# Casting a decoder's weights for scratch on GpSimd ahead of the first block

## The reference

```
xn   = rmsnorm(x) ; proj = xn @ w_in                 # 1024 -> 2048: B | C | xc | u
conv = B * causal_conv3(C * xc)                      # 512 channels
ssm  = GLU(Re(C_ssm h_t) + D u_t), h_t = Lbar h_{t-1} + Bbar u_t   # 32 groups, 64 states
x    = x + concat(conv, ssm) @ w_out                 # 1024 x 1024
hn   = rmsnorm(x)
x    = x + (silu(hn @ w_gate) * (hn @ w_up)) @ w_down   # 1024 x 2816, twice, and 2816 x 1024
y    = rmsnorm(x)
```

## Time and profile before

| | |
|---|---|
| time, median of 2 runs | 1637.3 us (1628.8 to 1645.8) |
| profiled execution | 1652.2 us |
| its span, slowest core (4) | 1650.3 us |
| spans of the 8 cores | 1614.6 to 1650.3 us |
| PE / DVE / ACT / Pool busy | 65% / 31% / 24% / 6% |
| mean rate of DMA | 114 GB/s |

### The profile page before, as it was taken

One profiled execution on the slowest core, in us unless ns is written; L12 is line 12 of the kernel. 1 busy time (PEld: TensorE's weight loads), 2 busy tenths in 40 slices (PEclk: granted clock), 3 DMA queues, 4 the chain that ended last, 5 costly groups with the idle time before them and its releaser, 6 DMA issues.

```text
span 1650.3 us, 23077 instructions; the slowest of 8 cores (1614.6 to 1650.3 us)
## 1 busy us (share of the span) xinstructions
PE 1066.9 (65%) x7740; PEld 560.6 (34%) x7740; DVE 511.4 (31%) x1071; ACT 391.5 (24%) x851; POOL 104.3 (6%) x187
## 2 busy tenths in 40 slices
PE   0343534345533357669897939898948899778992
PEld 0323324122210135343333624333724333453341
DVE  0117446235211154214515122532321551411111
ACT  0041433254421301331102151101132110132101
POOL 6010020200023000000000000000000000000000
PEclk9998656555555578869999959999977999998996
DMA  9450420678887321313344213345132334322442
GB/s 45 24 138 0 115 81 2 179 205 259 249 250 235 116 57 33 103 46 128 115 138 150 56 60 121 116 131 153 43 102 74 125 122 128 128 66 89 139 132 86
DMA packets 144387, 187.31 MB, mean 114 GB/s; under 512 B 13518, under 2 KB 106222, under 8 KB 144208
## 3 DMA queue, kind: packets, MB, share of 16 engines
q1 hardware_dynamic: 132800, 152.35, 32.3%
q0 software_dynamic: 11472, 33.49, 7.7%
HBM read 152.94 MB, written 32.85 MB: 113 GB/s over the span
## 4 chain that ended last, share of the span: by engine, by line
PE 40%; DMA 24%; DVE 16%; ACT 9%; issue 7%; POOL 2%; DVEq 1%; ACTq 0%; SPq 0%; POOLq 0%
PE bank L1011 13%; PE bank L1033 8%; DMA RGU<-wgu_s 4%; PE bank L749 3%; PE bank L914 3%; DMA STG<-wd 3%; ACT XN L672 3%; PE bank L925 3%; DMA STG<-wg 3%; DVE L2T L790 3%; DVE SETUPT L416 3%; DMA SETUPT<-ci 2%; PE bank L976 2%; DMA STG<-wu 2%; PE bank L771 2%
## 5 line engine op out<-in xcount | busy, mean ns | idle before, releaser
L1011 PE MATMUL bank<-SETUPT,RGU 128*128 128x512 bf16 (+1 forms) x1760 | 396.6, 370 | 103.1 <-ACT RGU L320 32.4
L1011 PEld LDWEIGHTS bank<-SETUPT,RGU 128*128 128x128 bf16 x1760 | 172.1, 104 | 326.4 <-issue 185.3
L749 PE MATMUL bank<-XTO,RWIN 128*128 128x512 bf16 (+1 forms) x640 | 166.4, 390 | 83.3 <-DMA RWIN<-win_s 24.8
L1033 PE MATMUL bank<-RW,ARENA 128*128 128x512 bf16 x748 | 183.0, 391 | 55.3 <-ACT RW L314 29.4
L1017 DVE TENSOR_TENSOR ARENA<-bank,SETUPT 128x512 bf16<-128x512 f32 (+1 forms) x110 | 66.3, 610 | 258.6 <-PE bank L1011 167.3
L749 PEld LDWEIGHTS bank<-XTO,RWIN 128*128 128x128 bf16 x640 | 64.1, 106 | 183.9 <-issue 144.1
L1033 PEld LDWEIGHTS bank<-RW,ARENA 128*128 128x128 bf16 x748 | 68.7, 98 | 168.5 <-issue 108.2
L691 PE MATMUL bank<-identb,XN 128*128 128x128 bf16 x272 | 34.4, 306 | 116.7 <-DVE XN L684 103.8
L1015 ACT ACTIVATE SETUPT<-bank 128x512 f32<-128x512 f32 (+1 forms) x110 | 57.0, 528 | 150.1 <-PE bank L1011 145.5
L976 PE MATMUL bank<-RW,ARENA 128*128 128x512 bf16 x272 | 67.0, 391 | 31.7 <-DVE RW L316 14.0
L1055 POOL DMA_DIRECT2D yp<-SETUPT x16 | 9.2, 578 | 1041.3 <-DVE SETUPT L1048 1039.8
(11 more groups left out here) (220 smaller groups left out, 1059.6 us busy)
## 6 DMA issues: line engine op xcount, KB each, us to landing
RGU<-wgu_s SPq DMA_DIRECT2D x88, 512.0 KB, 3.5
RW<-wd_s SPq DMA_DIRECT2D x176, 128.0 KB, 2.2
RWIN<-win_s SPq DMA_DIRECT2D x64, 256.0 KB, 2.7
STG<-wg SPq DMA_DIRECT2D x22, 512.0 KB, 7.4
STG<-wu SPq DMA_DIRECT2D x22, 512.0 KB, 6.0
wgu_s<-RGU POOLq DMA_DIRECT2D x22, 512.0 KB, 7.0
STG<-wd SPq DMA_DIRECT2D x44, 256.0 KB, 4.2
STG<-w_in SPq DMA_DIRECT2D x16, 512.0 KB, 5.0
```

What stands on the lines that cost most here:

```text
L749: E("pe", lambda e, bk=bk, wt=wt, k=k: e.matmul(bk[:, 0:NT], lhsT=wt[:, k, :], rhs=XTv[:, k, 0:NT], start=(k == 0), stop=(k == 7)), reads= ...
L1011: E("pe", lambda e, bk=bk, wt=wt, gi=gi, k=k: e.matmul(bk[:, 0:NT], lhsT=wt[:, gi, k, :], rhs=HT[:, k, 0:NT], start=(k == 0), stop=(k == 7 ...
L1033: E("pe", lambda e, bk=bk, wt=wt, f=f, t=t: e.matmul(bk[:, :], lhsT=ACT_[:, f * 512 + t * 128:f * 512 + (t + 1) * 128], rhs=wt[:, :], star ...
```

## The change

A section is added on Pool's queue, after the streams are set up and before any block is run. It loads in f32, casts on Pool and stores to scratch all of w_out (16 parts) and w_down (44 parts), and 15 of the 22 gate/up tiles (two parts each). Two staging buffers and one bf16 buffer for gate/up lie in the part of the arena that the decode block doesn't use; w_out and w_down parts are cast into RW's slots. The decode block then reads these weights from scratch, as the prompt blocks do, and casts only the first 7 gate/up tiles itself. The norm gain of the second norm is no longer multiplied into gate/up weights, but into HT at the transposes' eviction, in all blocks: eight `mul` instead of two `copy` on ACT per 128 tokens. The memsets of `prep_part1` and `prep_part3` go from Pool to DVE. Cut to its core:

```diff
-            Vx(lambda e: e.memset(BDR, 0.0), [], [b_bd], "pool")
+            Vx(lambda e: e.memset(BDR, 0.0), [], [b_bd])
...                                                 (11 memsets more, alike)
         def lookahead(stream, first, reqs, depth):
-            q = [stream.get(first, *reqs[i]) for i in range(min(depth, len(reqs)))]
+            fl = first if isinstance(first, list) else [first] * len(reqs)
+            q = [stream.get(fl[i], *reqs[i]) for i in range(min(depth, len(reqs)))]
...
+        GU_BG = 7
+        AR3 = ARENA[:, 0:4096].rearrange("p (r c) -> p r c", c=256)
+        bgst = [AR3[:, 0:8, 64:192], AR3[:, 8:16, 64:192]]
+        bggu = AR3[:, 0:16, 192:256].bitcast(BF16).rearrange("p (g k) c -> p g k c", g=2)
...
+        for key, pf, sap in wo_reqs():
+            bg_parts.append(("w", key, sap, pf(r_w.t[0])[0][1], 0, 1))
+        for key, pf, sap in wd_reqs():
+            bg_parts.append(("w", key, sap, pf(r_w.t[0])[0][1], 0, 1))
+        for key, pf, sap in gu_reqs()[GU_BG:]:
+            prt = pf(r_gu.t[0])
+            bg_parts.append(("g", key, sap, prt[0][1], 0, 2))
+            bg_parts.append(("g", key, sap, prt[1][1], 1, 2))
+
+        def bg_load(q):
+            kind_, key, sap, src_ap, pi, npart = bg_parts[q]
+            i = q % 2
+            if len(src_ap.shape) == 3:
+                view = bgst[i]
+            else:
+                view = bgst[i][:, 0:src_ap.shape[1] // 128, :]
+                src_ap = src_ap.rearrange("p (a c) -> p a c", c=128)
+            E("pool", lambda e: e.dma_start(out=view, in_=src_ap), writes=[b_bgst[i]], chan=bgst_ch[i])
+            return view
+
+        bg_views = {0: bg_load(0)}
+        for q in range(len(bg_parts)):
+            if q + 1 < len(bg_parts):
+                bg_views[q + 1] = bg_load(q + 1)
...
+            if kind_ == "w":
...
+                E("pool", lambda e, dst_ap=dst_ap, view=view: e.tensor_copy(out=dst_ap, in_=view),
+                  reads=[b_bgst[q % 2]], writes=r_w.b[si])
...
+                E("pool", lambda e, sap=sap, t=t: e.dma_start(out=sap, in_=t[:]), reads=r_w.b[si], writes=[sbuf],
+                  chan=r_w.sch[si])
+            else:
+                E("pool", lambda e, pi=pi, view=view: e.tensor_copy(out=bggu[:, pi, :, :], in_=view),
+                  reads=[b_bgst[q % 2]], writes=[b_bggu])
+                if pi == npart - 1:
...
+                    E("pool", lambda e, sap=sap: e.dma_start(out=sap, in_=bggu), reads=[b_bggu], writes=[sbuf],
+                      chan=bggu_ch)
...
+                        for kk in range(4):
+                            k = hh * 4 + kk
+                            E("act", lambda e, bk=bk, kk=kk, k=k, t=t: e.mul(
+                                out=DST[:, k, t * 128:(t + 1) * 128], in_=bk[:, kk * 128:(kk + 1) * 128],
+                                mul=gain[:, k:k + 1]), reads=[bb, b_G], writes=[b_dst])
...
             if kind == "p" and bi == 0:
+                handover(b_bgst + [b_bggu], mixer_bufs + b_actf)
...
-            norm_transpose(nt, HT, b_ht, 4, xt, bx)
+            norm_transpose(nt, HT, b_ht, 4, xt, bx, gain=G2C)
...
+            wo_it = lookahead(r_w, False, wo_reqs(), 3)
...
+            gu_it = lookahead(r_gu, [first and f < GU_BG for f in range(NF)], gu_reqs(), 1)
...
+            wd_it = lookahead(r_w, False, wd_reqs(), 3)
```

More of the change, by code:

```diff
@@ L453, in prep_part1 @@
             (r0, i0) = CHN[0]
-            Vx(lambda e: e.memset(BDR, 0.0), [], [b_bd], "pool")
-            Vx(lambda e: e.memset(NBDI, 0.0), [], [b_bd], "pool")
-            Vx(lambda e: e.memset(r0, 0.0), [], [b_bl[0]], "pool")
-            Vx(lambda e: e.memset(i0, 0.0), [], [b_bl[0]], "pool")
+            Vx(lambda e: e.memset(BDR, 0.0), [], [b_bd])
+            Vx(lambda e: e.memset(NBDI, 0.0), [], [b_bd])
+            Vx(lambda e: e.memset(r0, 0.0), [], [b_bl[0]])
+            Vx(lambda e: e.memset(i0, 0.0), [], [b_bl[0]])
             for ci_ in range(2):
-                Vx(lambda e, ci_=ci_: e.memset(CHN[1][ci_], 0.0), [], [b_bl[1]], "pool")
+                Vx(lambda e, ci_=ci_: e.memset(CHN[1][ci_], 0.0), [], [b_bl[1]])
             for ee in range(2):
@@ L528, in prep_part3 @@
         def prep_part3():
-            E("pool", lambda e: e.memset(KT[:], 0.0), writes=[b_kt])
-            V(lambda e: e.memset(K0F, 0.0), "pool")
+            E("dve", lambda e: e.memset(KT[:], 0.0), writes=[b_kt])
+            V(lambda e: e.memset(K0F, 0.0))
             for ci_ in range(2):
                 for cj_ in range(2):
-                    Vx(lambda e, ci_=ci_, cj_=cj_: e.memset(CHN[ci_][cj_], 0.0), [], [b_bl[ci_]], "pool")
+                    Vx(lambda e, ci_=ci_, cj_=cj_: e.memset(CHN[ci_][cj_], 0.0), [], [b_bl[ci_]])
             (r0, i0) = CHN[0]
@@ L660, in build_nc, with wo_reqs, gu_reqs @@
         mixer_bufs = [b_xt] + b_mix + b_zg
+        def wo_reqs():
+            return [(("wo", k, half), (lambda t, k=k, half=half: [(
+                t[:, :], wout_d[k * 128:(k + 1) * 128, half * 512:(half + 1) * 512], None)]),
+                wout_s[k, :, half * 512:(half + 1) * 512]) for half in range(2) for k in range(8)]
+        def gu_reqs():
+            return [(f, (lambda t, f=f: [
+                (t[:, 0, :, :], wg_d[:, f * 128:(f + 1) * 128].rearrange("(k p) c -> p k c", p=128), None),
+                (t[:, 1, :, :], wu_d[:, f * 128:(f + 1) * 128].rearrange("(k p) c -> p k c", p=128), None)]),
+                wgu_s[f, :, :, :, :]) for f in range(NF)]
@@ new lines, in wd_reqs @@
+        def wd_reqs():
+            return [(("wd", f, half), (lambda t, f=f, half=half: [(
+                t[:, :], wd_d[f * 128:(f + 1) * 128, half * 512:(half + 1) * 512], None)]),
+                wd_s[f, :, half * 512:(half + 1) * 512]) for half in range(2) for f in range(NF)]
+        GU_BG = 7
+        AR3 = ARENA[:, 0:4096].rearrange("p (r c) -> p r c", c=256)
+        bgst = [AR3[:, 0:8, 64:192], AR3[:, 8:16, 64:192]]
+        b_bgst = [Buf("bgst0"), Buf("bgst1")]
+        bgst_ch = [P.chan(), P.chan()]
@@ new lines, in build_nc @@
+        bg_wslot = [None]
+        for q in range(len(bg_parts)):
+            if q + 1 < len(bg_parts):
+                bg_views[q + 1] = bg_load(q + 1)
+            kind_, key, sap, src_ap, pi, npart = bg_parts[q]
+            view = bg_views.pop(q)
+            if kind_ == "w":
+                si = r_w.i % r_w.n
+                r_w.i += 1
+                t = r_w.t[si]
+                dst_ap = t[:, :].rearrange("p (a c) -> p a c", c=128)
+                E("pool", lambda e, dst_ap=dst_ap, view=view: e.tensor_copy(out=dst_ap, in_=view),
+                  reads=[b_bgst[q % 2]], writes=r_w.b[si])
+                sbuf = Buf("scr_RW_%s" % (key,))
+                scr_bufs[("RW", key)] = sbuf
+                E("pool", lambda e, sap=sap, t=t: e.dma_start(out=sap, in_=t[:]), reads=r_w.b[si], writes=[sbuf],
[4 more added lines that the diff above has]
+                if pi == npart - 1:
+                    sbuf = Buf("scr_RGU_%s" % (key,))
+                    scr_bufs[("RGU", key)] = sbuf
+                    E("pool", lambda e, sap=sap: e.dma_start(out=sap, in_=bggu), reads=[b_bggu], writes=[sbuf],
+                      chan=bggu_ch)
@@ L678, in rmsnorm_stats_all, with norm_transpose @@
             E("dve", lambda e: e.reciprocal(out=cols, in_=cols), reads=[b_ss], writes=[b_ss])
-        def norm_transpose(nt, DST, b_dst, colbase, xt, bx, do_stats=True):
+        def norm_transpose(nt, DST, b_dst, colbase, xt, bx, do_stats=True, gain=None):
             if do_stats:
@@ L693, in norm_transpose @@
                             start=True, stop=True), reads=[b_xn, b_identb], writes=[bb], signal=(kk == 3))
-                    E("act", lambda e, bk=bk, hh=hh, t=t: e.copy(
-                        out=DST[:, hh * 4:hh * 4 + 4, t * 128:(t + 1) * 128],
-                        in_=bk[:, :].rearrange("p (k c) -> p k c", k=4)), reads=[bb], writes=[b_dst])
+                    if gain is None:
+                        E("act", lambda e, bk=bk, hh=hh, t=t: e.copy(
+                            out=DST[:, hh * 4:hh * 4 + 4, t * 128:(t + 1) * 128],
+                            in_=bk[:, :].rearrange("p (k c) -> p k c", k=4)), reads=[bb], writes=[b_dst])
+                    else:
+                        for kk in range(4):
[3 more added lines that the diff above has]
+                                mul=gain[:, k:k + 1]), reads=[bb, b_G], writes=[b_dst])
         blocks = [("s", 0)] + [("p", i) for i in range(4)]
@@ L1023, in do_block @@
             yield "gudone"
-            wd_it = lookahead(r_w, first, [(("wd", f, half), (lambda t, f=f, half=half: [(
-                t[:, :], wd_d[f * 128:(f + 1) * 128, half * 512:(half + 1) * 512], None)]),
-                wd_s[f, :, half * 512:(half + 1) * 512]) for half in range(2) for f in range(NF)], 3)
+            wd_it = lookahead(r_w, False, wd_reqs(), 3)
             for half in range(2):
```

12 lines of the change are left out of this document (4 added, 8 removed).

## The result

The changed kernel takes 1863.4 us (median of 12 executions), the kernel before 1641.1 us (median of 10): 1.135 times the time before, 95% interval 1.130 to 1.140. Times here are medians of all executions; ratios and their intervals leave out the slow ones, in which as a rule half of the chip was granted a lower clock.

What follows compares the result with a forecast made beforehand. The start was taken as bound by loading and rewriting weights, with ACT waiting for Pool's scratch stores. 1652 + 523 (stall) - 92 (savings) + 11 (additions) = 2094 us, stated as 2080 because the profiled execution was slow; range 1880 to 2200.

Steps and rivals of the forecast that it cites:

- The stall: Decode block's start: ACT stops at the third w_in cast until Pool's section lets the first win_s store go; +523 us.
- The section's length: Pool's background section: starts at 69 us, 519 for pieces, 40 for casts, so it ends at 628 us.
- 519 us: Transfers of Pool's background section: 99,840 pieces at 5.2 ns each on the software queue.
- tiles at 12 us: Sign in Pool's section: gate/up tiles at 12 us, not 21 to 26, would show the price per piece wrong.
- the first rival: Pool's section: engines' pace and buffers, not pieces, set its length; w part 3.05 us, tile 12.5, time 1895 us; chance 0.20.
- LI's landing: Setup load on Pool's queue, 2,048 pieces of 4 B: 11.5 us, 5.6 ns each, taken as support for the piece price.
- the section's start: Pool's queue: background loads can't move data before 69 us, behind small setup loads.
- The savings: Decode block's later weight stages read scratch: w_out -10, gate/up -48, w_down -34, sum -92 us.
- their cheaper casts give nothing: Decode block's gate/up: the seven tiles still cast there are bound by DMA and stay at 42 us.
- The gain on ACT: Second-norm evictions: eight muls for two copies; +0.7 to +2.5 us per prompt block, about 1 in decode, 8 in all.
- a small ACT pass from a bank takes 0.26 us and eight muls in a row 2.46: Second-norm eviction on ACT: the step pricing eight muls at 2.06 to 2.46 us per token tile.
- DVE's memsets: Table preparation: six memsets of 0.5 us join DVE's chain in prep_part1, +3 us; those of prep_part3 cost 0.

Runs made afterwards that it cites:

- one slot: The changed kernel with the background's bf16 gate/up tile in one RGU slot (4 KB rows, 128-piece store) instead of the arena's gaps: 1.118 of the kernel before.
- two slots: The changed kernel with the background's bf16 gate/up tile in RGU's two slots in turn instead of the arena's gaps: 1.122 of the kernel before.
- the split gain: The changed kernel with DVE multiplying the first of two banks of each second-norm transpose and ACT's four muls the second: 1.121 of the kernel before.

## Why the prediction was right in kind and wrong in size

- *The stall.* Right: the first `win_s` store behind the whole section on Pool, ACT stopped at the third w_in tile, PE and DVE with it, an unchanged mixer of 190 us afterwards. PE stood at zero in six of the 40 slices, not in some ten, since the stall was shorter. The three runs that moved stores or shortened the section moved the stall as the order of the queue says.
- *The section's length: this is the step that failed,* its term "519 us", the price of 5.2 ns per piece. From the first load's landing to the last store's issue the section took about 325 us, against 519 and 40 more for casts that wait: w parts 3.0 us (predicted 3.3 to 4.3), tiles 10 (21 to 26). The prediction had named tiles at 12 us as the sign that this price is wrong, and they came at 10. The runs with one slot and with the arena's buffer compare 128 pieces with 2,048 in the same store: 4.2 and 5.6 us, 0.7 ns per piece, a seventh of the price (against the 3.2 us of the run with two slots it would be 1.25). The loads' pieces were not varied; a tile's 4,096 pieces in 10.0 us bound the price of any of them at 2.4 ns in the mean. What sets the pace is what the first rival had: two buffers and a landing for a w part (3.05 us predicted, 3.0 measured), one buffer for a tile (12.5 predicted, 10.0 measured). The rival's 1895 us was the nearer number, and I had given it 0.20. The Trainium skill (DMA: Bandwidth & Descriptors, section Anatomy of one DMA — SWDGE (gpsimd) path) gives 2.0 us plus bytes/436 GB/s; by it I estimate 2.6 us for a w load and 3.2 us for 512 KB. Measured were 3.4 us, and from 3.2 (the stores with two slots) to 6.5 us (the loads of w_up), so it is mostly too low here. The Trainium skill's page calls the generation of descriptors small; the trace agrees as far as it goes, since 1,920 pieces more made the store only 1.4 us longer.
- *Where the price came from.* From one core in one execution. The profile is of core 4, the slowest, and LI's landing there isn't that of most others. LI's landing on core 4 and on core 0:

```profile
DMA to landing us min/median/max: 22.2/22.2/22.2
```

```profile
DMA to landing us min/median/max: 16.9/16.9/16.9
```

  On six of the eight cores LI landed in 14.5 to 16.9 us (cores 4 and 5: 22.2 and 21.4), and PE's first matmul, which waits for the last small load, started at 49 us on core 0, not 69. So 11.5 us for LI's pieces were 5.6 on core 0 (2.7 ns each, with 12.5 us for LR), and the section's start (51 us) was 18 us too late in my sum as well. The first matmul on core 4 and on core 0:

```profile
68.96 3.65 PE L582 MATMUL bank<-identf,SETUPT 64*128 64x64 f32 x16 [68.96 <-DMA SETUPT<-ci]
```

```profile
49.36 3.65 PE L582 MATMUL bank<-identf,SETUPT 64*128 64x64 f32 x16 [49.36 <-DMA SETUPT<-ci]
```

  Nor is it a property of core 4: in the changed kernel's profile LI lands there in 14.3 us and no core is late, and in the run with all stores on ACT cores 0 and 1 are (21.5 and 23.1 us). Six of the 13 profiled executions have one such pair, 4 and 5 or 0 and 1, its first matmul comes some 20 us later, and in each of the six the slowest core is one of the two. On core 4 the third cast therefore moved by 270 us (108 to 378), of which the late start hid 20.

  Even 2.7 ns per piece of 4 B was no price for pieces of 256 and 512 B. I had taken the row that was nearest in kind and outlying in place over the rows nearest in size.
- *The savings.* -92 predicted, -95 measured on core 0: w_out -9 (-10), gate/up -45 (-48), w_down -41 (-34); in the mean of the cores -9, -47 and -41. Working from landings and slots was right here, and was nearer for the section too (the first rival). One step in it was wrong without harm: "their cheaper casts give nothing". Without the gain 22 tiles' casts gave 8 us in the run that did this alone, so the seven tiles should give 2 or 3.
- *The gain on ACT.* +8 predicted for the evictions; they cost 29 us in the prompt blocks and 4 in the decode block, and the run that did it alone lost 27 net of what its casts gained. The step "a small ACT pass from a bank takes 0.26 us and eight muls in a row 2.46" took the price from one pass and from muls that read SBUF. A mul from a bank with the gain lasts 0.37 us and the next starts 0.09 us after its end, 0.457 us in all; the casts' muls from SBUF last 0.39 us and start 0.29 us apart, so they overlap. A token tile costs 3.6 us, not 2.06 to 2.46.
- *DVE's memsets.* +3 predicted; the mixer's length did not change (190 us in the mean of the cores in both).
- *Sum with what was measured:* 295 - 95 + 36 = 236 us on core 0, against 523 - 92 + 11 in the forecast; in the mean of the cores 286 - 97 + 31 = 220 us.

What is open: why muls from a bank don't overlap, and why a pair of cores starts late; why the prompt blocks' loss differs by core (36 us on core 0, 23 on core 3, 31 in the mean, of which the muls explain 29); and whether gate/up beside the background is slow by the DMA engines' share alone (0.88 of their time), which no run separates.

## What to carry to other kernels

Work put "in the background" on an engine's queue delays everything that stands behind it there, also the few small DMAs that somebody needs; list them, and the buffers that both sides pass through, before the work itself is priced. Move those few first, and the background is worth something: 0.979 against 1.135, of which 0.015 is the split gain. Then ask what its bytes share with what runs beside it, and read a price that carries a forecast on more than one core and in more than one execution.

## What the runs showed that I had not expected

DVE's multiplications with two inputs in SBUF get slower while Pool casts. In the mixer of the kernel before and of the one with all stores on ACT, both on core 3, from 110 to 300 us:

```profile
L416 DVE TENSOR_TENSOR SETUPT<-SETUPT,L1R 128x512 f32<-128x512 f32 x30 | 20.8, 692 | 3.0
```

```profile
L416 DVE TENSOR_TENSOR SETUPT<-SETUPT,L1R 128x512 f32<-128x512 f32 x30 | 23.3, 777 | 3.0
```

692 against 777 ns in the mean for the same form. The mean hides two kinds. In the second kernel, on the same core:

```profile
145.06 1.71 DVE L416 TENSOR_TENSOR SETUPT<-SETUPT,L1I 128x512 f32<-128x512 f32 x2
145.47 0.74 POOL L724 CAST RW<-ARENA 128x512 bf16<-128x512 f32 x1
146.79 0.56 POOL L728 DMA_DIRECT2D wd_s<-RW  x1 [0.57 <-POOL RW L724]
146.87 0.69 DVE L416 TENSOR_TENSOR SETUPT<-SETUPT,L1R 128x512 f32<-128x512 f32 x1
```

Beside a cast, the two take 1.71 us; beside Pool's issue of a store, the next takes 0.69 as ever. Over the eight cores, 251 of these multiplications overlap no Pool cast and take 691 to 694 ns, though the DMA engines are at 0.63 of their time in this stretch; the 229 that overlap one take 888 ns in the mean and up to 1604. So it is the casts, not the DMA traffic. Copies of DVE out of a bank (128x64: 225 ns) are as fast beside a cast as without. Added up over the mixer, DVE's instructions beside casts are 14 us longer than their forms' shortest, per core, of the 19 us by which the mixer is longer in that kernel: an estimate of how much of the stretch is DVE's.

The Trainium skill (GPSIMD Engine Reference, section Specifications) says that GpSimd shares its SBUF interfaces with VectorE, with contention for DVE instructions that have two SBUF inputs or run in a 2-port mode; for two SBUF inputs the trace agrees. In the changed kernel itself this costs nothing, since DVE stands still while Pool casts.
